# A split copy of x that keeps x's column order, with every eighth column taken at the weight load instead of at the copy

## The reference

```python
x = layer_norm(ALPHA * x + h, ln1_g[i], ln1_b[i])
f = moe(x, ...)            # 64 routed SwiGLU experts, top 8 per token, one shared expert
x = layer_norm(ALPHA * x + f, ln2_g[i], ln2_b[i])
# inside moe, for a block of tokens that go to expert e:
h = x_pad[tok]
y = (jax.nn.silu(h @ w_gate[e]) * (h @ w_up[e])) @ w_down[e]
```

## Time and profile before

| what | value |
|---|---|
| median of 3 runs | 1386.18 us (1386.15 to 1387.7) |
| the profiled execution, its own time | 1388.24 us |
| span of its trace | 1386.5 us |
| mean granted TensorE clock | 0.988 |
| TensorE matmul busy | 1347.8 us (97%) |
| TensorE weight load busy | 800.3 us (58%) |
| VectorE busy | 564.2 us (41%) |
| ScalarE busy | 357.3 us (26%) |
| mean DMA rate | 338 GB/s |

### The profile page before, as it was taken

One profiled execution on the slowest core, in us unless ns is written; L12 is line 12 of the kernel. 1 busy time (PEld: TensorE's weight loads), 2 busy tenths in 40 slices (PEclk: granted clock), 3 DMA queues, 4 the chain that ended last, 5 costly groups with the idle time before them and its releaser, 6 DMA issues.

```text
span 1386.5 us, 19138 instructions
## 1 busy us (share of the span) xinstructions
PE 1347.8 (97%) x7240; PEld 800.3 (58%) x7240; DVE 564.2 (41%) x1123; ACT 357.3 (26%) x607; POOL 10.2 (1%) x24
## 2 busy tenths in 40 slices
PE   8999999999999999997999999999999999999996
PEld 8986445445445445436999997544454454454452
DVE  5756223322323322234577666423323233233234
ACT  4433111212211222113554442222122112122110
POOL 0000000000000000000000000000000000000000
PEclk9999999999999999998999999999999999999998
DMA  9765699999999999974444454479999999999991
GB/s 331 274 256 218 264 382 421 422 422 423 422 422 422 421 422 422 422 290 193 183 182 177 161 228 196 165 278 404 422 422 422 422 421 423 422 421 422 421 422 50
DMA packets 82767, 468.45 MB, mean 338 GB/s; under 512 B 7065, under 2 KB 19481, under 8 KB 32674
## 3 DMA queue, kind: packets, MB, share of 16 engines
q1 hardware_dynamic: 81296, 463.50, 82.4%
q10 hardware_dynamic: 1426, 4.33, 0.8%
HBM read 466.76 MB, written 1.05 MB: 337 GB/s over the span
## 4 chain that ended last, share of the span: by engine, by line
PE 95%; DVE 2%; issue 1%; ACT 1%; DMA 0%; POOL 0%; DVEq 0%; POOLq 0%; ACTq 0%
PE ps L578 32%; PE ps L600 17%; PE ps L678 10%; PE ps L536 9%; PE ps L556 9%; PE ps L690 6%; PE ps L712 5%; PE ps L761 2%; PE ps L586 1%; PE ps L615 1%; PE ps L522 1%; PE ps L543 1%; PE ps L745 1%; PE ps L754 1%; DVE acc L1088 0%
## 5 line engine op out<-in xcount | busy, mean ns | idle before, releaser
L578 PE MATMUL ps<-ring,xsT 128*64 128x512 f32 x2048 | 450.1, 592 | 1.7 <-DVE slot_tok L1064 1.7
L578 PEld LDWEIGHTS ps<-ring,xsT 128*64 128x64 f32 x2048 | 146.9, 137 | 293.0 <-issue 291.2
L600 PE MATMUL ps<-ring,hidT 128*64 128x512 f32 x1024 | 237.2, 606 | 2.3 <-ACT hidT L860 2.3
L1070 DVE SCALAR_TENSOR_TENSOR gated<-sig,slot_gate,ps 128x256 f32<-128x256 f32 x64 | 30.7, 480 | 364.7 <-ACT sig L856 364.7
L1002 DVE TENSOR_TENSOR ring_low<-ring,wh 128x1024 fp32r<-128x1024 f32 (+1 forms) x112 | 128.3, 1148 | 105.1 <-ACT wh L838 104.6
L1079 DVE TENSOR_TENSOR yl<-ps,yh 128x512 fp32r<-128x512 f32 x128 | 88.5, 691 | 169.2 <-ACT yh L865 169.2
L838 ACT CAST wh<-ring 128x1024 fp32r<-128x1024 f32 (+1 forms) x112 | 110.4, 988 | 156.5 <-PE ps L678 66.8
L600 PEld LDWEIGHTS ps<-ring,hidT 128*64 128x64 f32 x1024 | 68.6, 138 | 128.0 <-issue 124.4
L865 ACT CAST yh<-ps 128x512 fp32r<-128x512 f32 x128 | 74.9, 585 | 241.9 <-PE ps L600 241.9
L856 ACT ACTIVATE sig<-ps 128x256 f32<-128x256 f32 x64 | 24.6, 384 | 405.2 <-PE ps L578 405.2
L536 PE MATMUL ps<-sel,xh 128*128 128x256 f32 x512 | 127.8, 292 | 0.0
(11 more groups left out here) (150 smaller groups left out, 1270.9 us busy)
## 6 DMA issues: line engine op xcount, KB each, us to landing
ring<-in_w_gate SPq DMA_DIRECT2D x128, 1024.0 KB, 10.2
ring<-in_w_up SPq DMA_DIRECT2D x128, 1024.0 KB, 12.2
ring<-in_w_down SPq DMA_DIRECT2D x128, 1024.0 KB, 11.8
ring<-in_b_w_in SPq DMA_DIRECT2D x8, 3072.0 KB, 11.0
ring<-in_a_w_in SPq DMA_DIRECT2D x12, 1024.0 KB, 12.3
ring<-in_b_w_out SPq DMA_DIRECT2D x4, 3072.0 KB, 10.4
ring<-in_a_w_out SPq DMA_DIRECT2D x1, 3072.0 KB, 16.7
ring<-in_sh_gate SPq DMA_DIRECT2D x2, 1024.0 KB, 4.9
```

What stands on the lines that cost most here:

```text
L578: last = nc.tensor.matmul(ps[64 * half:64 * half + 64, p, :], xsT[:, c, (2 * p + half) * SLOTS:(2 * p + half + 1) * SLOTS], slot_gu(s)[:, ...
L600: last = nc.tensor.matmul(ps[64 * half:64 * half + 64, 4 + h, :], hidT[:, p, kk * P + 64 * half:kk * P + 64 * half + 64], slot_dn(s)[:, kk ...
```

## The change

`xh` and `xl` get the plain layout of x. The four copies (two on ACT, two on DVE, over both layers four of each) read and write contiguously. The gather's 1024 weight loads read every eighth element, a step of 32 bytes, where they read adjacent ones. Sizes, addresses of the tiles, the number of instructions, their order and all waits stay as they are.

```diff
-        xh = sb("xh", [P, TT, KC, P], FP32R)
-        xl = sb("xl", [P, TT, KC, P], FP32R)
+        xh = sb("xh", [P, TT, D], FP32R)
+        xl = sb("xl", [P, TT, D], FP32R)
...
-                            last = nc.tensor.matmul(dst, part[:, t, c, :], sel[:, t, :], start=(n == 0), stop=(n == 3))
+                            last = nc.tensor.matmul(dst, part[:, t, c:D:KC], sel[:, t, :], start=(n == 0), stop=(n == 3))
...
-                    nc.scalar.copy(xh[:, t], x_tok[:, t, :].rearrange("p (q c) -> p c q", c=KC)).then_inc(W.xh_ready, 1)
+                    nc.scalar.copy(xh[:, t, :], x_tok[:, t, :]).then_inc(W.xh_ready, 1)
...
-                    nc.vector.tensor_tensor(xl[:, t], x_tok[:, t, :].rearrange("p (q c) -> p c q", c=KC),
-                                            xh[:, t].bitcast(FP32), ALU.subtract).then_inc(W.xl_ready, 1)
+                    nc.vector.tensor_tensor(xl[:, t, :], x_tok[:, t, :],
+                                            xh[:, t, :].bitcast(FP32), ALU.subtract).then_inc(W.xl_ready, 1)
```

## The result

The changed kernel takes 1518.52 us (median, 1517.89 to 1520.26) against 1386.82 us beside it: a ratio of 1.0951, 95% interval 1.0932 to 1.0970. It is 131.7 us slower, where no difference was forecast.

The account below looks back on a forecast made before the run. TensorE's stream was taken to bound the kernel. Loads 0 plus copies 0 on a profiled 1388.24 us, which lies 2.1 us above the runs' median, gave a forecast median of 1386.2 us, range 1384.7 to 1392 us.

Parts of the forecast that it names:

- What bounds the kernel: Experts' stage: TensorE's stream is the path, 97% busy, 95% of the chain; each ns added there adds to the time.
- The step of a gather product: Gather: 116 ns a product, 1024 of them 119 us; a load needs 111.6 ns, so 4.4 ns to spare.
- Part 1, the loads: Gather's weight loads with a step of 32 bytes: free by L513's row, cost 0 on the path.
- The bound from hid and shid: Gather loads: if any step costs 10 to 19 ns more, as their records suggest, +5.7 to +15.0 us.
- Rival 2: Gather loads pay for a step what ACT and DVE pay: 216 ns a load, +102 us, 1488 us; chance 0.04.
- Part 2, the copies: Contiguous copies before the experts: 4.2 us less on ACT, 3.2 us less on DVE, all hidden, 0 on the path.
- Rivals 3 and 4: Copies: shorter ones are on the path, at most 7.4 us faster (0.03); or don't get shorter, 1386.2 us (within forecast's 0.83).
- rival 1: Each of the 1024 gather loads pays a little for the step: 1391.9 to 1401.2 us; chance 0.10.

Follow-up runs that it names:

- the run of forms: Kernel before plus 96 extra calls at its start: transposes and plain products of an identity matrix, operands adjacent or 8 elements apart; 1415.83 us in one run.

## Why the prediction was wrong

**What bounds the kernel** was right: each ns on a gather product came out on the path, 129.9 us of 130.1 us of span.

**The step of a gather product** was right as far as the runs tell: a load had at most a few ns to spare, and step 2, at 120.6 ns against 116, already shows. Whether 4.4 ns were there is open. They rest on L754's 111.6 ns; beside 128 moving float32 columns adjacent loads came every 116 ns (L678 of the run of forms).

**Part 1, the loads,** is the step that failed: "By this row the step is free". It read L513 at 193 ns as the float32 load with step 8, laid it beside xh's adjacent 189 ns, and found no difference. But L513 loads in transpose mode, and the right neighbour, an adjacent load in that mode, takes 140 ns (L672 above). The two were nearly equal by chance: the mode saved about 50 ns and the step cost 53. The other half of the reading, 110 ns a step, was the pace of the transposes' stream and could not show what their loads cost. The prediction named the transpose as a doubt, beside the type and the number of moving columns, and gave it no number. It put the term at 0; the runs showed 240.6 - 116 = 124.6 ns a product and 129.9 us in all. The bound from hid and shid had the same flaw: both are transposes, and their step is 2. The loads of xh with step 2, as products, have medians of 194 and 195 ns, 6 to 7 more than adjacent.

**Rival 2** (0.04) is what happened: the load pays for the step what ScalarE and VectorE pay. It priced 216 ns a load and +102 us; measured were 240.6 ns and +129.9 us. The mechanism is right, the term mis-sized: it doubled 0.81 ns a column to 1.62, where a column on a line of its own takes 240.6/128 = 1.88 ns. The Trainium skill ("Advanced Engine Details and Errata", SBUF Cachelines), cited there, says that accesses on different 16-byte lines pay, and that at least two hits on a line absorb the latency of the access. The runs agree: step 4, one hit a line, takes 235 ns, and step 2, two hits, 120.6. The prediction let one row of another kind of instruction overrule it.

**Part 2, the copies,** was right in size (1.05 and 1.23 us) and in worth: nothing, by the run with the copies alone. Rivals 3 and 4 are out, and rival 1 as well: a step of 8 costs far more than its 19 ns.

**What stays open**: why step 16 is 18 ns cheaper than step 8, by what transpose mode loads faster, and what a step of 2 costs in it (hid's 199 ns lie above the 193 of step 8, but its loads come in pairs, right behind a wait). No version here beats the kernel before. Its rearranged copy, paid four times and hidden, is the right place for the step: 7 us of ScalarE and VectorE, off the path, instead of 130 us on it.

## What to carry to other kernels

Put a rearrangement where an operand is written once, not where TensorE loads it hundreds of times: for a plain product, estimate the pace of weight loads at the larger of the adjacent pace, the stream's and some 1.85 ns for each 16-byte line that a load opens (1.74 to 1.88 here). For a stepped moving operand there is one row, 229/128 = 1.79 ns a line. Before a row is taken as the price of an operation, ask whether it is the same kind of instruction, and find the row of that kind without the feature; a likeness across kinds proves nothing. Two float32 columns per line are nearly free (here 0.34%); one is not. By the rule above it would be hidden only beside a stream of over 240 ns, which no run here shows.

## What the runs showed of the hardware

- Weight loads of plain products, 128 four-byte columns each, follow each other every 116 ns or less when adjacent, every 120.6 ns with step 2, 175.6 with 3, 235 with 4, 240.6 with 8 and 222.5 with 16; fp32r and float32 pay alike (238 ns between float32 loads with step 8).
- With step 8 the pace is 238.6 ns at a granted clock of 1.00 and 240 ns at 0.50.
- In transpose mode the load record is 140 ns adjacent and 193 ns with step 8, against 192 and 335 ns for a product.
- A product with a stepped moving operand (float32, 128 columns, step 8) takes 229 ns a pass, against 116 ns adjacent.
- A float32 pass streams 256 columns in 216 ns, an fp32r product in 116 ns.
- With 64 moving columns instead of 256 beside the same stepped loads, the mean granted clock fell from 0.989 to 0.902 and the time rose from 1518.5 to 1592.6 us.
